# Dense products that read their moving operand and write their results from the last column to the first

## What is computed

```python
def swiglu(h, w_gu, w_down):
    gate, up = jnp.split(h @ w_gu, 2, axis=-1)
    return (jax.nn.silu(gate) * up) @ w_down
...
proj = h @ w_in[i]
...
x = x + jnp.square(jax.nn.relu(hf @ w_ff1[i])) @ w_ff2[i]
```

## Time and profile before

| | us |
|---|---|
| median of 3 runs | 1607.84 |
| lowest and highest | 1607.14, 1609.78 |
| the profiled execution | 1607.01 |
| its span, first to last instruction | 1605.0 |
| PE busy in the span | 1536.2 (96%) |
| DVE busy | 1064.6 (66%) |
| ACT busy | 730.3 (46%) |

### The profile page before, as it was taken

How to read it: one execution, slowest core, us unless ns; L and a number is a source line. 1 busy time by engine, 2 the same in 40 slices (tenths; PEclk the granted TensorE clock), 3 DMA queues, 4 the chain that set the end, 5 groups by cost and what they waited for, 6 DMA issues and landing times. The chain is left out here.

```text
span 1605.0 us, 36127 instructions
## 1 busy us (share of the span) xinstructions
PE 1536.2 (96%) x15669; PEld 1478.2 (92%) x15669; DVE 1064.6 (66%) x1277; ACT 730.3 (46%) x814; POOL 69.9 (4%) x52
## 2 busy tenths in 40 slices
PE   7999989999999999999998999999997889999998
PEld 6999989878999999999988999999886778999997
DVE  5766487764867547664677766467768776777436
ACT  5443345543534344433446433354565444555333
POOL 2000000100100001000101000021000000100000
PEclk9999999999999999999999999999999999999999
DMA  8665545201556556555533555564320012555552
GB/s 269 189 192 201 185 157 169 96 2 51 183 188 193 200 184 184 183 184 187 181 131 96 182 187 191 185 201 145 120 79 3 3 56 81 184 184 189 202 186 79
DMA packets 155065, 243.26 MB, mean 152 GB/s; under 512 B 9283, under 2 KB 106174, under 8 KB 154814
## 3 DMA queue, kind: packets, MB, share of 16 engines
q1 hardware_dynamic: 154510, 240.63, 45.7%
q10 hardware_dynamic: 432, 0.79, 0.2%
HBM read 240.34 MB, written 1.05 MB: 150 GB/s over the span
## 5 line engine op out<-in xcount | busy, mean ns | idle before, releaser
L2888 DVE TENSOR_TENSOR w_lo<-raw,w_hi 128x2048 fp32r<-128x2048 f32 x225 | 522.9, 2335 | 243.0 <-ACT w_hi L2715 242.1
L2518 PE MATMUL dense_ps<-h_hi,w_hi 128*128 128x256 f32 x2368 | 668.3, 282 | 12.2 <-DVE h_lo L2963 8.6
L2519 PE MATMUL dense_ps<-h_lo,w_hi 128*128 128x256 f32 x2368 | 662.0, 280 | 0.0
L2520 PE MATMUL dense_ps<-h_hi,w_lo 128*128 128x256 f32 x2368 | 662.0, 280 | 0.0
L2715 ACT ACTIVATE w_hi<-raw 128x2048 fp32r<-128x2048 f32 x225 | 428.5, 1913 | 332.6 <-DMA raw<-in_ffn_w_down 116.2
L2518 PEld LDWEIGHTS dense_ps<-h_hi,w_hi 128*128 128x128 f32 x2368 | 450.5, 190 | 18.3 <-issue 17.8
L2519 PEld LDWEIGHTS dense_ps<-h_lo,w_hi 128*128 128x128 f32 x2368 | 447.4, 189 | 0.8 <-issue 0.5
L2520 PEld LDWEIGHTS dense_ps<-h_hi,w_lo 128*128 128x128 f32 x2368 | 448.1, 189 | 0.0
L2520 PE MATMUL dense_ps<-g_hi,w_lo 128*128 128x256 f32 x960 | 266.9, 278 | 0.0
L2518 PE MATMUL dense_ps<-g_hi,w_hi 128*128 128x256 f32 x960 | 266.9, 278 | 0.0
L2519 PE MATMUL dense_ps<-g_lo,w_hi 128*128 128x256 f32 x960 | 266.9, 278 | 0.0
(11 more groups left out here) (554 smaller groups left out, 1750.5 us busy)
## 6 DMA issues: line engine op xcount, KB each, us to landing
raw<-in_ffn_w_gu SPq DMA_DIRECT2D x176, 512.0 KB, 4.6
raw<-in_ffn_w_down SPq DMA_DIRECT2D x88, 512.0 KB, 4.1
raw<-in_w_ff SPq DMA_DIRECT2D x64, 512.0 KB, 4.2
raw<-in_w_in SPq DMA_DIRECT2D x36, 512.0 KB, 4.4
raw<-in_a_w_in SPq DMA_DIRECT2D x32, 512.0 KB, 4.3
raw<-in_a_w_out SPq DMA_DIRECT2D x8, 512.0 KB, 4.0
raw<-in_b_w_in SPq DMA_DIRECT2D x8, 512.0 KB, 4.2
raw<-in_b_w_out SPq DMA_DIRECT2D x8, 512.0 KB, 4.1
```

What stands on the lines that cost most here:

```text
L2518: pe.matmul(o, hi, mh, start=start, stop=False)
L2519: pe.matmul(o, hi, ml, start=False, stop=False)
L2520: return pe.matmul(o, lo, mh, start=False, stop=stop)
L2888: dve.tensor_tensor(w_lo[:, p % SLOTS, :], raw[:, p % SLOTS, :], w_hi[:, p % SLOTS, :].bitcast(F32), ALU.subtract).then_inc(lo_ready, 1)
```

## The change

One line is added to the helper `three`: the output, and both halves of the moving operand, are taken with their second axis reversed. Column 255 is read first and its result written first, column 0 last. Output column j still receives the products of moving column j, and the three products still accumulate in the same order, so the computed values are the same. Weight tiles are read as before. All 10,800 products of the run go through this helper. The instruction list of every engine keeps its instructions, their number, their order and their waits; in the built program these matmuls have a step of -1 where they had +1 in the moving operand and in the output. Every source line below moves down by one.

```diff
@@ -2515,6 +2515,7 @@
         def _(pe):
             def three(o, hi, lo, mh, ml, start, stop):
 
+                o, mh, ml = o[:, ::-1], mh[:, ::-1], ml[:, ::-1]
                 pe.matmul(o, hi, mh, start=start, stop=False)
                 pe.matmul(o, hi, ml, start=False, stop=False)
                 return pe.matmul(o, lo, mh, start=False, stop=stop)
```

## The result

The changed kernel takes 1631.4 us (median of four runs, 1630.2 to 1632.2) against 1607.5 us before: a ratio of 1.0155, 95% interval 1.0125 to 1.0184. It is slower by 24 us, or 1.5%. All four runs lie above the slowest of the 67 runs of the kernel before that were taken in all, 1622.0 us. The forecast was no change, with the doubling as the main rival; it is neither.

What follows compares the result with a forecast made beforehand. PE was taken as the bound, through 10,800 dense products. Read, write and rhythm each added zero to the 1605.0 us span; with the profiled execution's 2 us and the median's 0.8 us the forecast was 1607.8 us, range 1604 to 2700 us.

Steps and rivals of the forecast that it cites:

- the doubling: Rival: a backward column costs twice a forward one, each product going from 115.5 to about 213 ns, 2661 us; chance 0.27.
- What bounds the kernel: PE, busy for 96% of the span; 10,800 dense products at a mean 115.5 ns make 1247 us of 1605 us.
- The write, taken at zero: Term: writing and accumulating into PSUM backwards in the dense products adds 0 us.
- The read, taken at zero: Term: reading the moving operand of the dense products backwards adds 0 us.
- VectorE's merge: Line 521 on DVE: starts 0.57 us apart with runs of 2, 0.33 us with runs of 4; few neighbours are punished.
- my bounds, 0 and 98 ns: Price range per backward product: zero, like a forward product's 113.3 ns, up to 98 ns, from line 2627's 213 ns.
- The rhythm, taken at zero: Term: products keep the same one of PE's two distances, 113.3 or 117.8 ns, in each stretch; 0 us.
- the spread of three runs, 2.6 us: Evidence for the rhythm term: the three runs' spread says each start repeats itself from run to run.
- the case that every stretch is slow: Rival: the three fast long stretches fall into the slow rhythm, adding 19 us, 1627 us; chance 0.10 with a fixed price.
- a fixed price: Rival: each backward matmul costs 4.5 ns more, 49 us in all, 1656 us; chance 0.10 with the slow-rhythm case.
- my bound of 0.2%: Claim that 3.2 us is about what a measurement of this kernel can tell from no change; chance of that 0.55.
- The control that I named: Sign: the projection at line 637 keeps its direction among reversed products, its 283 ns unchanged under doubling.

Runs made afterwards that it cites:

- e2: Kernel before, with only the output written backwards and the moving operand read forwards: 1611.2 us, ratio 1.0017.
- e8: Kernel before, moving operand alone read in groups of four columns, groups ascending, each group backwards: 1604.2 us, ratio 0.9987.
- e1: Kernel before, with only the moving operand read backwards and the output written forwards: 1633.2 us, ratio 1.0148.
- e7: Kernel before, moving operand alone read in groups of four columns, each forwards, last group first: 1630.2 us, ratio 1.0138.
- e13: Kernel before, moving operand alone read as columns 127 down to 0, then 255 down to 128: 1633.9 us, ratio 1.0184.
- e16: Kernel before, moving operand alone read in groups of 16 columns, each forwards, last group first: 1632.6 us, ratio 1.0176.
- e17: Kernel before, moving operand alone read in groups of 16 columns, groups ascending, each group backwards: 1790.6 us, ratio 1.1161.
- e5: Changed kernel plus a forward 64-column matmul ahead of the first product of each narrow-job chunk and each wide job: 1643.5 us, ratio 1.0218 to the kernel before.
- e11: Kernel before, moving operand alone read in groups of 64 columns, each forwards, last group first: 1602.0 us, ratio 1.0008.
- e12: Kernel before, with only the first of the three products reading its moving operand backwards, all writes forwards: 1648.2 us, ratio 1.0269.
- e4: Kernel before plus a 64-column matmul ahead of the first product of each narrow-job chunk and each wide job: 1627.0 us, ratio 1.0112.
- e3: Kernel before, moving operand and output both taken as columns 128 to 255, then 0 to 127, forwards: 1602.5 us, ratio 0.9979.
- e14: Kernel before, forwards, with all products but those of the first and last contraction tile using 64 of 128 weight columns: 1596.7 us, ratio 0.9961.

## Why the prediction was wrong, point by point

**What bounds the kernel** was right, and so was the multiplier: 10,800 products, so a nanosecond each is 10.8 us. Two slips changed nothing: 1497 matmuls in 170 us, less two or three, are 113.8 ns and not 113.6 at most, and 1053 us is 10,800 x 97.5 ns. That nothing else moves was right too: DVE, ACT and POOL kept their busy times to within 1.4 us.

**The write, taken at zero:** right (e2: 1.0017, interval across 1). The rule of the Trainium skill's "PSUM — Partial Sum Buffer" (Specifications (TRN2)) on non-contiguous patterns does not reach a backward run here: e2's last stretch holds the same 113.3 ns per product.

**The read, taken at zero:** this is the step that failed. I argued from VectorE's merge that neighbours in a run are what counts, and that the backward operand visits the same groups of four. The first half of that holds: e8 reverses inside each four for nothing. The Trainium skill's "SBUF — State Buffer" (Door 1: The DMA port swizzle) agrees with it as far as it goes, for accesses within one 16-byte line. It says nothing of the order of the lines, and my reading that by it a backward read costs nothing went further than the page. What I left out is that the order of the groups themselves has a price. Going down through them is one portion of about 4.5 ns per product against the fast rhythm (e1, e7, e13, e16) and nothing against the slow one, and the order of e17 costs 20 ns. At 53% of the products that is the 25 us that this term should have held. No row of the trace before had a descending order; my bounds, 0 and 98 ns, held the true value, but I took an end.

**The rhythm, taken at zero:** also wrong, in two ways. I had seen the two distances and priced the case that every stretch is slow at 1627 us, where 1631 was measured; the 4 us are the fast pieces outside the three long stretches. It was this case that came. But I took it for a matter of chance and gave it, together with a fixed price, 0.10. It is no chance, and no term apart from the read: the backward read removes the fast rhythm (e5: an extra irregular start in 72 chunks and 12 wide jobs, and none leads back to it). In the other way, I took the spread of three runs, 2.6 us, as proof that the rhythm repeats from run to run. It does not: more runs of the kernel before lie between 1593 and 1622 us. For this kernel my bound of 0.2% for what can be told from no change was too fine.

**The doubling** did not happen, and nothing near it. The control that I named, line 637, kept its 283 ns, but durations are the same in both rhythms and could show nothing. Its distances can: the matmuls of lines 637 to 639, read forwards, start 119 to 121 ns apart before, right behind products at 113 ns, and 115 to 121 ns apart after. They were not slowed.

**Shown and not shown.** Shown: the backward read alone makes the loss; it takes away the fast rhythm; it does not shrink with a shorter weight load; the step of -1 between neighbours within a four is free (e8), and 15 or more steps down between groups (e16, e7) cost what the change costs; the price comes in one portion. Not settled: what mechanism is behind it, whether three descents (e11) are free and fifteen (e16) cost all by their number or by the length of the runs, what makes e17 dear, why mixed directions (e12) are dearer than one, and what chooses between the two forward rhythms after a wait.

## What to carry to other kernels

Where TensorE is the bound, read its cost as the distance between starts and look for more than one value of it at the same shape and clock: a change may not touch the values and yet remove the better one. Keep moving operands ascending through memory, or at least in forward runs of 64 columns, and all in the same direction; reversing the output in PSUM was free here, so a reversal that is needed belongs on the write. Before a change of one per cent is judged, learn from a dozen runs how far the old kernel varies by itself.

## What the runs showed of the hardware

- At full granted clock a 128 x 128 by 128 x 256 float32r product follows the last after 113.3 ns or 117.8 ns on average, in stretches that last for a hundred microseconds and more; an irregular start moves PE from one to the other (e4).
- With the moving operand descending the 113.3 ns never occur; the distance is 117.8 ns on average, mostly as a repeating 118, 120, 115 (the kernel after, e1). With forward groups of 4 or 16 columns taken from the end (e7, e16) they never occur either; with groups of 64 or 128 (e11, e3) or with each four reversed (e8) they do.
- With the output descending the 113.3 ns do occur (e2).
- Columns in groups of 16, each backwards, groups ascending: 133.4 ns (e17).
- One backward read among two forward ones: 119.5 ns on average (e12).
- With 64 weight columns in place of 128 the fast forward distance stays 113.4 ns, and 8% of the threes take 353 ns in place of 45% (e14).
